# Hybrid decoder step: router with tokens on partitions, a threefold last block in the gather, keys and values loaded one per unit

## What is computed

```python
x += W_out [ HGRN2 heads || gated MLP groups ](RMSNorm(x))      # recurrent state per sample sequence
x += CrossAttn_4heads(RMSNorm(x), memory K/V)                   # cached K/V per sample sequence
logits = t @ w_router + b_router                                # t = RMSNorm(x), 288 tokens
top_v, top_e = top_k(logits, 4); gates = softmax(top_v)         # 4 of 32 experts
x += sum over chosen experts of gate * (swiglu(t @ w1[e] + b1[e]) @ w2[e] + b2[e])
y = RMSNorm(x) * g_final
```

## Time and profile before

| | us |
|---|---|
| median of three runs (lowest, highest) | 1297.99 (1297.44, 1299.78) |
| the profiled execution | 1298.86 |
| its span | 1297.1 |
| busy in the span: PE, DVE, ACT, POOL | 1189.5, 405.0, 228.9, 56.7 |
| moved by DMA | 467.04 MB, 360 GB/s over the span |

### The profile page before, as it was taken

How to read it: one execution, slowest core, us unless ns; L and a number is a source line. 1 busy time by engine, 2 the same in 40 slices (tenths; PEclk the granted TensorE clock), 3 DMA queues, 4 the chain that set the end, 5 groups by cost and what they waited for, 6 DMA issues and landing times.

```text
span 1297.1 us, 16693 instructions
## 1 busy us (share of the span) xinstructions
PE 1189.5 (92%) x6756; PEld 602.3 (46%) x6756; DVE 405.0 (31%) x815; ACT 228.9 (18%) x356; POOL 56.7 (4%) x81
## 2 busy tenths in 40 slices
PE   7999998969399999999999999999999999999985
PEld 5778797948343434434343343423333333334231
DVE  3655666346812121221213212121213212121203
ACT  4342233221311111111011111101111111111012
POOL 5202001010300000000000000000000000000000
PEclk9999999998699999999999999999999999999998
DMA  9832397498579999999999999999999999999992
GB/s 314 257 106 89 108 293 259 162 334 315 222 281 429 427 427 428 428 428 428 428 428 428 428 428 428 428 428 428 428 428 428 429 428 428 428 428 428 429 428 96
DMA packets 79860, 467.04 MB, mean 360 GB/s; under 512 B 4368, under 2 KB 50992, under 8 KB 55024
## 3 DMA queue, kind: packets, MB, share of 16 engines
q1 hardware_dynamic: 72816, 455.36, 85.7%
q0 software_dynamic: 1616, 6.65, 1.6%
q10 hardware_dynamic: 5392, 4.54, 1.1%
HBM read 460.84 MB, written 5.70 MB: 360 GB/s over the span
## 4 chain that ended last, share of the span: by engine, by line
PE 67%; DMA 25%; DVE 4%; ACT 3%; issue 1%; SPq 0%; DVEq 0%; ACTq 0%
PE bank L1639 22%; DMA ring<-w 22%; PE bank L1673 13%; PE bank L1289 9%; PE bank L1614 5%; PE bank L1594 5%; PE bank L1456 4%; PE bank L1444 2%; PE bank L1658 1%; DMA ring<-w_xo 1%; DMA ring<-w_out 1%; ACT rest L743 1%; DVE split L968 1%; ACT split L637 1%; ACT rest L727 1%
## 5 line engine op out<-in xcount | busy, mean ns | idle before, releaser
L1639 PE MATMUL bank<-ring,rest 128*64 128x512 f32 x2048 | 453.8, 594 | 16.8 <-DMA ring<-w 15.2
L1639 PEld LDWEIGHTS bank<-ring,rest 128*64 128x64 f32 x2048 | 143.8, 137 | 306.7 <-issue 262.4
L1673 PE MATMUL bank<-ring,rest 128*64 128x512 f32 x1024 | 226.8, 595 | 16.4 <-ACT rest L743 16.4
L1225 DVE TENSOR_SCALAR rest<-bank 128x512 f32<-128x512 f32 x32 | 22.1, 692 | 509.3 <-PE bank L1639 509.3
L1673 PEld LDWEIGHTS bank<-ring,rest 128*64 128x64 f32 x1024 | 70.7, 137 | 151.1 <-issue 127.9
L1204 DVE TENSOR_TENSOR rest<-rest,bank 128x512 f32<-128x512 f32 (+1 forms) x102 | 66.9, 680 | 220.2 <-PE bank L1614 220.1
L1289 PE MATMUL bank<-rest,ring 128*128 128x288 f32 (+1 forms) x512 | 124.9, 404 | 8.6 <-DMA ring<-w_in 8.6
L1289 PEld LDWEIGHTS bank<-rest,ring 128*128 128x128 f32 x512 | 97.8, 192 | 33.1 <-DMA ring<-w_in 8.6
L739 ACT ACTIVATE rest<-rest 128x512 f32<-128x512 f32 x32 | 20.2, 631 | 498.0 <-DVE rest L1225 498.0
L1614 PE MATMUL bank<-rest 128*128 128x512 f32 (+1 forms) x204 | 98.4, 611 | 1.3 <-ACT rest L751 1.3
L1456 PE MATMUL bank<-split 128*128 128x288 f32 x576 | 83.8, 307 | 7.6 <-DVE split L1009 4.4
(11 more groups left out here) (297 smaller groups left out, 696.5 us busy)
## 6 DMA issues: line engine op xcount, KB each, us to landing
ring<-w SPq DMA_DIRECT2D x192, 2048.0 KB, 30.3
ring<-w_in SPq DMA_DIRECT2D x12, 1024.0 KB, 12.0
ring<-k_t SPq DMA_DIRECT2D x8, 1024.0 KB, 12.6
ring<-v_c SPq DMA_DIRECT2D x8, 1024.0 KB, 6.4
ring<-w_xk SPq DMA_DIRECT2D x4, 1024.0 KB, 5.0
ring<-w_xv SPq DMA_DIRECT2D x4, 1024.0 KB, 5.0
ring<-w_out SPq DMA_DIRECT2D x4, 1024.0 KB, 8.2
ring<-w_xq SPq DMA_DIRECT2D x4, 1024.0 KB, 12.1
```

What stands on the lines that cost most here:

```text
L1639: last = t.matmul(out, slots[:, k, :], w[:, col], start=False, stop=(k == KT - 1))
L1673: last = t.matmul(ps[2][CAP * ds:CAP * ds + CAP, :], actT[:, at:at + CAP], w[:, b, 512 * ds:512 * ds + 512], start=(a == 0 and b == 0), st ...
```

## The change

- The state reads loop over sequences first, heads inside.
- A key load follows each of w_out's units 2 and 3 and of w_xq's first three. Values 0 to 2 go to slots 10, 6 and 7, values 3 to 5 and the other keys to the slots of w_xq and w_out, values 6 and 7 and w_xo to the slots of keys. The first expert loads wait for other units accordingly. ScalarE's casts of w_xo wait for the values in their slots.
- The router has tokens on partitions: three products per chunk, the last over a threefold copy of the 32 sample tokens (POOL copies it). ScalarE squares each chunk as it comes, POOL adds the squares, six products with ones give the sums per token.
- The normalised rows are split without the gain of the norm (it is applied where the gathered tokens are copied from PSUM): ScalarE makes high and middle parts, VectorE both subtractions, by halves of 512 columns. The third token block holds its three parts on 96 partitions, one matmul for three: 56 per gather instead of 72. The first gather runs by halves.
- The chosen experts are found by replacing the top four values and comparing, instead of by indices; one instruction makes a pair's one-hot rows instead of six.
- The gathered tokens are copied half by ScalarE (four copies with the gain), half by VectorE.
- The count is read and the branch taken before the last combine; without further rounds the last squares stand beside the last sums.

```diff
-EARLY = 5
+LATE_SLOT = [SLOTS - 5 + k for k in range(5)] + [4, 5, 0] + [10, 6, 7] + [1, 2, 3] + [11, 12] + [13, 14, 4, 5]
...
+            return u % PRE if u < U_KC else LATE_SLOT[u - U_KC]
...
+        def further_rounds(eng, fullest, one_round, before=nothing, behind=nothing, otherwise=nothing):
             with eng.If(fullest > CAP):
+                before()
                 one_round(1)
...
+                behind()
             with eng.Else():
-                pass
+                otherwise()
...
-                    for k in range(EARLY):
-                        load_unit(U_KC + k)
...
+                if U_XV + PRE <= u < U_XV + PRE + 5:
+                    load_unit(U_KC + u - U_XV - PRE)
+            for u, before in ((U_KC + 5, U_OUT + 2), (U_KC + 6, U_OUT + 3), (U_KC + 7, U_XQ), (U_VC + 3, U_XQ + 1),
+                              (U_VC, U_XQ + 1), (U_VC + 4, U_XQ + 2), (U_VC + 1, U_XQ + 2), (U_VC + 5, U_XQ + 3),
+                              (U_VC + 2, U_XQ + 3), (U_VC + 6, U_KC), (U_VC + 7, U_KC + 1), (U_XO, U_KC + 2),
+                              (U_XO + 1, U_KC + 3), (U_XO + 2, U_KC + 5), (U_XO + 3, U_KC + 6)):
+                wait_unit_used(sp, before)
+                load_unit(u)
...
-            for u, j in ((U_VC + 2, 12), (U_VC + 5, 6), (U_VC + 7, 8), (U_XO + 1, 14), (U_XO + 2, 0),
-                         (U_XO + 3, 2), (U_XO + 3, 4), (U_XO + 3, 10)):
+            for u, j in ((U_VC + 3, 10), (U_VC + 5, 12), (U_XO, 6), (U_XO + 1, 8), (U_XO + 2, 0),
+                         (U_XO + 3, 2), (U_XO + 3, 4), (U_XO + 3, 14)):
...
+            pool.dma_start(gain_k.rearrange("p (q r) -> p q r", r=2),
+                           ffn_g.rearrange("(q p r) -> p q r", p=P, r=2)).then_inc(gain_in, 16)
...
-            pool.dma_start(frow, ffn_g.partition_broadcast(P)).then_inc(frow_in, 16)
-            pool.wait_ge(y_sq, 2 * TT)
-            pool.memset(hx[:, :, 2, :], 0.0).then_inc(hx_zero, 1)
-            for tt in range(TT):
-                R = ROWS[tt]
-                pool.wait_ge(h_hi, tt + 1)
-                pool.tensor_tensor(htmp[tt][0:R], htmp[tt][0:R], hx[0:R, 0, tt, :], ALU.subtract).then_inc(h_rest, 1)
+            pool.wait_ge(mv_out, 16)
+            for k in range(KT):
+                pool.wait_ge(x_add, KT + k + 1)
+                pool.tensor_copy(copies(x_c, k), xT[:, k, SEQ:T].unsqueeze(1).to_broadcast([P, COPIES, TS])).then_inc(xc_done, 1)
+                if k in (0, KT - 1):
+                    continue
+                pool.wait_ge(rsq_done, k + 1)
+                if k > 1:
+                    pool.wait_ge(rsq_sum, k - 1)
+                pool.tensor_tensor(sq_r[:, 0, :], sq_r[:, 0, :], sq_r[:, k, :], ALU.add).then_inc(rsq_sum, 1)
+            pool.wait_ge(proj, 64)
+            pool.memset(outp[1], 0.0).then_inc(outp_done, 2)
             pool.wait_ge(outp_done, 2)
             pool.dma_start(outp[1][0:NE], b2).then_inc(b2_in, 16)
-            pool.wait_ge(h_tok, TT)
+            pool.wait_ge(h_split, 2 * TT)
...
+                act_e.wait_ge(kv_used, DECB + i - 11)
...
+            act_e.wait_ge(mv_out, 16)
+            for k in range(KT):
+                act_e.wait_ge(x_add, KT + k + 1)
+                a.activation(sq_r[:, k, :], xT[:, k, :], ACT.Square).then_inc(rsq_done, 1)
+                if k == 1:
+                    upper_unit(15)
+            a.activation(copies(sq_c, 1), xT[:, KT - 1, SEQ:T].unsqueeze(1).to_broadcast([P, COPIES, TS]),
+                         ACT.Square).then_inc(rsq_done, 1)
+            act_e.wait_ge(rsq_sum, KT - 2)
+            a.copy(copies(sq_c, 0), sq_r[:, 0, SEQ:T].unsqueeze(1).to_broadcast([P, COPIES, TS])).then_inc(rsq_done, 1)
+            act_e.wait_ge(rss_ps, 1)
+            act_e.wait_ge(act_step, 2)
+            for tt in range(TT):
+                R = ROWS_C[tt]
+                a.activation(yrs[0:R, tt:tt + 1], ps[L_BANK[tt]][0:R, NE:NE + 1], ACT.Sqrt, bias=eps[0:R],
+                             scale=1.0 / D).then_inc(y_std, 1)
+            act_e.wait_ge(yrs_done, 1)
+            act_e.wait_ge(y_ev, TT)
+            for tt in range(TT):
+                R = ROWS_C[tt]
+                a.activation(hx_hi[tt][0:R, 0:512], y[0:R, tt, 0:512], ACT.Copy, scale=yrs[0:R, tt:tt + 1]).then_inc(h_hi, 1)
+            for tt in range(TT):
+                R = ROWS_C[tt]
+                act_e.wait_ge(y_ps, TT + tt + 1)
+                a.activation(hx_hi[tt][0:R, 512:D], ps[Y_BANK[TT + tt]][0:R, :], ACT.Copy,
+                             scale=yrs[0:R, tt:tt + 1]).then_inc(h_hi, 1)
+            for tt in range(TT):
+                R = ROWS_C[tt]
+                a.copy(y[0:R, tt, 512:D], ps[Y_BANK[TT + tt]][0:R, :]).then_inc(y_ev, 1)
+            def middle_part(n):
...
+                act_e.wait_ge(h_rest, n + 1)
+                if tt < 2:
+                    a.copy(hx[:, 1, tt, q], htmp[tt][:, q]).then_inc(h_mid, 1)
+                else:
+                    a.copy(hx_c[0:2 * TS, q], htmp[tt][0:2 * TS, q]).then_inc(h_mid, 1)
             for n in range(2 * TT):
+                middle_part(n)
             act_e.wait_ge(gate_in, 1)
             a.activation(gate, gate, ACT.Exp).then_inc(gate_exp, 1)
             def evac_gather(nth, parity):
                 act_e.wait_ge(xg_ps, 2 * nth - 1)
-                a.copy(q[:, 0:512], ps[4][:, :]).then_inc(xg_done, 1)
-                act_e.wait_ge(xg_ps, 2 * nth)
-                a.copy(q[:, 512:1024], ps[5][:, :]).then_inc(xg_done, 1)
+                for k in range(KT // 2):
+                    last = a.activation(xg[parity][:, k, :], ps[4][:, k * P:(k + 1) * P], ACT.Copy, scale=gain_k[:, k:k + 1])
+                last.then_inc(xg_done_a, 1)
...
+            def roots_beside_sums():
+                for tt in range(TT):
+                    act_e.wait_ge(comb_free, 2 * TT * PAIRS + 2 * tt + 2 + len(COMB_BANK))
+                    root_of_rows(tt)
+            further_rounds(act_e, fullest, one_round, behind=roots_behind_rounds, otherwise=roots_beside_sums)
...
+            dve.wait_ge(y_std, TT)
+            v.reciprocal(yrs, yrs).then_inc(yrs_done, 1)
+            dve.wait_ge(yrs_done, 1)
...
+                last = v.max(top[:, tt, :], logit[:, tt, 0:NE])
             link(last)
-            link(v.tensor_copy(topf, topi.bitcast(U32)))
-            v.tensor_tensor(gate, top[:, :, 0:TOPK], top[:, :, 0:1].to_broadcast([P, TT, TOPK]),
+            v.tensor_tensor(gate, logit[:, :, 0:NE], top[:, :, 0:1].to_broadcast([P, TT, NE]),
                             ALU.subtract).then_inc(gate_in, 1)
+            link(v.memset(top[:, :, TOPK:8], LOWEST))
             for tt in range(TT):
-                last = v.tensor_tensor(pick_t[:, tt], iota_e.unsqueeze(1).to_broadcast([P, TOPK, NE]),
-                                       topf[:, tt, 0:TOPK].unsqueeze(2).to_broadcast([P, TOPK, NE]), ALU.is_equal)
+                R = ROWS_C[tt]
+                last = v.match_replace(replaced[0:R, tt, :], top[0:R, tt, :], logit[0:R, tt, :], -LOWEST)
             link(last)
-            link(v.tensor_reduce(gates, pick_t.rearrange("p t k e -> p t e k"), AX, ALU.add))
-            v.tensor_tensor(chosen, gates, valid, ALU.mult).then_inc(chosen_done, 1)
+            v.tensor_tensor(chosen, replaced[:, :, 0:NE], logit[:, :, 0:NE], ALU.not_equal).then_inc(chosen_done, 1)
...
+            def select_pair(e):
+                v.tensor_tensor(sel.rearrange("p t (a s) -> p t a s", a=2),
+                                iota_slot[:, 0:CAP].unsqueeze(1).unsqueeze(1).to_broadcast([P, TT, 2, CAP]),
+                                place[:, :, bass.ds(e, 2)].unsqueeze(3).to_broadcast([P, TT, 2, CAP]),
+                                ALU.is_equal).then_inc(sel_done, 1)
...
+            def evac_gather(nth, parity):
+                dve.wait_ge(xg_ps, 2 * nth)
+                v.tensor_tensor(xg[parity][:, KT // 2:KT, :], ps[5][:, :].rearrange("p (k s) -> p k s", s=P),
+                                gain_k[:, KT // 2:KT].unsqueeze(2).to_broadcast([P, KT // 2, P]),
+                                ALU.mult).then_inc(xg_done_v, 1)
...
+            def rest_part(n):
...
+                dve.wait_ge(h_hi, n + 1)
+                if half:
+                    dve.wait_ge(y_ev, n + 1)
+                v.scalar_tensor_tensor(htmp[tt][0:R, q], y[0:R, tt, q], yrs[0:R, tt:tt + 1], hx_hi[tt][0:R, q],
+                                       ALU.mult, ALU.subtract).then_inc(h_rest, 1)
+            def third_part(n):
...
+                dve.wait_ge(h_mid, n + 1)
+                out, mid = (hx[:, 2, tt, q], hx[:, 1, tt, q]) if tt < 2 else (hx_c[0:R, q], hx_c[0:R, q])
+                v.tensor_tensor(out, htmp[tt][0:R, q], mid, ALU.subtract).then_inc(h_split, 1)
+            for half in range(2):
+                for tt in range(TT):
+                    rest_part(TT * half + tt)
+                for tt in range(TT):
+                    third_part(TT * half + tt)
...
+            def sums_end():
```

(40 more changed lines are left out.)

285 lines of the change are left out of this document (122 added, 163 removed).

## The result

The changed kernel takes 1255.96 us (median of four runs, 1253.99 to 1256.93) against 1298.01 beside it: ratio 0.967, 95% interval 0.9656 to 0.9686. The profiled span went from 1297.1 to 1255.1 us.

The account below looks back on a forecast made before the run. Bound: the 428 GB/s expert weight stream, so its start without holes and what follows its end count. Terms 3.3 + 5.4 + 7.1 + 1.2 + 11.4 + 5.5 = 33.9 off 1298.86 give 1265.0, by the median 1264.1; said 1264.5, range 1258 to 1279.

Parts of the forecast that it names:

- State reads: L1380's 64 matmuls, going round the heads, take 3.4 us at L1500's rate: 3.3 us gained, 4.7 at half of it.
- Keys one per unit: In w_out, fewer key loads ahead of its last unit end the last chunk at 217.0, not 222.4: 5.4 gained, ends 3 and 6.5.
- Values and w_xo: Earlier loads let ScalarE cast w_xo before copying o_x: 7.1 us gained, cover 0.5, plus 1.2 of 1.9 in the 72 matmuls.
- Router and split: Last residual add to first expert matmul takes 19.7 us, not 31.6: 11.9 gained, less 0.5 for lower clock, 11.4.
- The second item of its sum: Behind the last add: logits, top-8, small operations, counts on TensorE, then place, select and pick, put at 8.5 us.
- Tail: After the experts, branch ahead of the sums and squares beside matmuls: 5.5 us gained, 3.1 if TensorE pays for its branch.
- Expert loop: In the expert loop, shorter work per pair gains nothing, since all stays below the stream's 58.8 us per pair.
- rival 4: Expert loop becomes the bound from 58.8 us per pair; a pair of 61.1 eats the whole gain: 1302, chance 0.03.
- Rivals 1 and 2: Loads still late, 1271 to 1277, chance 0.12; split bound by ScalarE or longer logits chain, 1268.5 to 1271, chance 0.14.
- Rival 3: POOL's new reads hold VectorE up in the w_xo stage: 1267 to 1270, chance 0.08.
- hole: An earlier first expert pair could fill a hole of 1 or 2 us; counted for the range's low end only.

Follow-up runs that it names:

- experiment 2: The changed kernel with the 32 state reads per pass going head by head again: 1260.17 us, 4.2 later than 1255.96.
- Experiment 1: The changed kernel with all five key loads issued ahead of the last w_out unit again: 1264.04 us, 8.1 later than 1255.96.
- experiment 7: The kernel before, with unused extra matmuls (9, 3, 28, 5 calls) in TensorE's waits at w_xq and w_xo: 1294.85 us against 1299.01, ratio 0.9958.
- experiments 4 and 5: The changed kernel with VectorE's count read behind the sums: 1259.39 us; with that, squares behind sums, and keys, state reads, w_xo loads undone: 1284.32 us.

## Why the prediction was right, and where it was wrong

The direction, the places and most of the mechanisms were right; the gain was 8.1 us larger than forecast. By stages of the two profiles the keys give 3.6 us of this, router and split 1.5, the state reads 1.4, the w_xo stage 1.0 and the 72 matmuls at its head 0.6, with small gains in the loop and the tail; the start takes 1.3 back.

- **State reads:** forecast 3.3, the stage gained 4.65 (117.42 less 106.16 before, 114.05 less 107.44 after). Right mechanism, and the upper bound of its range was the value: 0.030 us per matmul, little above half of L1500's 0.053, with half its columns. Undone, it costs 4.2. By the rule of the Trainium skill that was weighed there (TensorE: Matmul & The Clock Gate, "The mechanism" of Part 3) nothing would have been gained; experiment 2 decides against it here, since the order of column groups alone makes 1.93 of 5.93 us, and 1.77 of 5.77 for the weight loads.
- **Keys one per unit: the step that failed.** Forecast 5.4 with ends of 3 and 6.5, priced up to the last chunk of w_out. To that point 6.4 came (the last add, forecast near 217.0, is at 216.1 when the stage's earlier start is taken out). But the stage behind it, w_xq, also began in that stall: 168 matmuls from 24.55 to 22.59 and 0.6 less between last add and first of them. Together 9.0, outside the stated ends. Experiment 1 gives 6.1 and 7.9 for the two points, experiment 7 gives 0.9 of it back at the 168 matmuls without touching a load. The step that failed is that this wait was priced only by its idle time. The lower clock behind it was put at nothing without a reason, although the same prediction charged 1.2 us for it at w_xo and the earlier trace rows showed 0.50 in another stage. The runs show 2.6 us there, 2.0 of them in the 168 matmuls that began at 0.50.
- **Values and w_xo:** forecast 7.1 for o_x's copy, measured 7.16, and the cover of 0.5 us was 0.53. For the 72 matmuls 1.2 of 1.9 was taken; this profile shows 1.8; the 11.3 us of five profiles in ten would have been 0.3.
- **Router and split:** forecast 19.7 us from last add to first expert matmul, measured 18.7; the gain 12.9 for 11.4. Half a microsecond of lower clock at the experts' start was subtracted and did not come; the split ended 15.6 us behind the add, not 16.5. The w_xo stage, taken at nothing, gave 1.0 (blocks of 3.79 us for 3.99). (The second item of its sum adds up to 8.6, not 8.5, and twelve times 0.6 is 7.2, not 7.3: together nothing.) Which of the many edits here gave how much is argued from rows and not tested.
- **Tail:** 5.5 forecast, 5.7 measured; 3.3 of it is the branch, 1.9 the squares (experiments 4 and 5). TensorE's own branch costs nothing here: the combine waits 1.28 us for ScalarE's copy in both kernels.
- **The start** lost 1.28 us in this profile: the first 16 matmuls took 7.15 us for 5.80. The experiments, which leave the start as it is, have 5.59 to 7.10, so this varies from one execution to the next and is no effect of the change.
- **Expert loop:** forecast at nothing, and it gave 0.6 us. But rival 4's point was wrong: the cover ends at 57.3 us per pair, not 58.8, and a pair of 61.1 would have cost some 60 us, not 37. Before, with the first expert matmul at 359.02, the same division gives 57.4, 1.4 us above the pair of 56.00.
- **Rivals 1 and 2** (late loads, a split bound by ScalarE) did not occur: no wait for w_out or w_xo is left. **Rival 3:** POOL's copies beside VectorE do stretch (up to 2.4 us, 0.26 alone), but no wait for them stands in the chain.

The time fell 2.0 us below the range. Its low end was built from three upper ends (state reads 1.4, router 1.5, hole 2 at most), which take 1264.5 to 1259.6 and not to the stated 1258; neither the upper end of the keys nor the clock behind their wait is in it. With both, 1.1 and 2.6 us, the same sum comes to 1255.9. Luck had little part in the miss: the 72 matmuls fell on their fast side and the start on a slow one, which nearly cancels.

## What to carry to other kernels

Price a removed wait to the end of the stage behind it: look at the granted clock of the slices behind the wait, and take the same matmuls at the other level from a stage without one. In this loop, bound by a stream that starts ahead, the cover was the time it really has divided by its turns, not the stream's time per turn; work out both. Before filling a wait, measure one filler: the same call can be two instructions.

## What was not expected of the hardware

- Matmuls that nobody uses made the kernel before 0.4% faster (1294.85 for 1299.01), in part by holding the granted clock at 1.00 through a wait of 7.65 us (9.77 us for 11.57 in the matmuls behind it); twice as many made it 0.2% slower.
- The same 72 matmuls, behind a wait of 1.7 us, took about 9.76 us in five profiles and about 11.30 in five others, with nothing between, in programs that do not differ there.
- A VectorE operation of 96 elements takes 1.85 us when POOL has begun 0.15 us before it.
